# Banded attention of a two-block transformer kernel: single heads in a row against batches of four heads

## The reference

```
WINDOW = 128; SWA_Q_HEADS = 8; SWA_KV_HEADS = 2; SWA_GROUP = 4; HEAD_DIM = 64
kb, vb = band(k), band(v)        # own block of 128 keys and the one before
s = einsum('bnqhgd,bnkhd->bnhgqk', qb, kb) * (HEAD_DIM ** -0.5) + bias
s = where(mask, s, NEG_INF)      # banded and causal
p = softmax(concatenate([s, sink], axis=-1), axis=-1)[..., :-1]
o = einsum('bnhgqk,bnkhd->bnqhgd', p, vb)
```

## Time and profile before

| | us |
|---|---|
| median of 3 runs (2503.61 to 2506.11) | 2503.81 |
| span of the profiled execution, first to last instruction | 2500.4 |
| median less span | 3.4 |
| banded attention, first weight load of its scores (269.08) to first weight load of the dense scores (358.25) | 89.17 |
| PE, DVE and ACT busy in it | 79.26, 81.90, 52.35 |

### The profile page before, as it was taken

How to read it: one execution, slowest core, us unless ns; L and a number is a source line. 1 busy time by engine, 2 the same in 40 slices (tenths; PEclk the granted TensorE clock), 3 DMA queues, 4 the chain that set the end, 5 groups by cost and what they waited for, 6 DMA issues and landing times.

```text
span 2500.4 us, 32413 instructions
## 1 busy us (share of the span) xinstructions
PE 2411.0 (96%) x11302; PEld 1886.2 (75%) x11302; DVE 1599.2 (64%) x2478; ACT 1248.2 (50%) x1874; POOL 751.4 (30%) x396
## 2 busy tenths in 40 slices
PE   8999899999999999999999999999997999999996
PEld 6587567778788878878788778766764878878885
DVE  4033887756563357675442734687247999999998
ACT  4111555434543432443333411377245888888887
POOL 0312100114444477334466331120311132123310
PEclk9999999999999999999999999999998999999998
DMA  6210000022222264222233211000438999999996
GB/s 241 98 49 3 35 1 1 1 101 87 91 93 101 95 241 151 84 85 91 93 118 112 73 61 40 34 1 1 153 141 309 402 395 388 380 391 385 392 390 234
DMA packets 86602, 384.08 MB, mean 154 GB/s; under 512 B 7980, under 2 KB 9180, under 8 KB 71520
## 3 DMA queue, kind: packets, MB, share of 16 engines
q1 hardware_dynamic: 81744, 365.25, 38.7%
q0 software_dynamic: 4752, 17.43, 2.6%
HBM read 361.60 MB, written 21.05 MB: 153 GB/s over the span
## 4 chain that ended last, share of the span: by engine, by line
PE 49%; issue 11%; DVE 7%; POOL 4%; ACT 2%; DMA 1%; SPq 0%; POOLq 0%; DVEq 0%; ACTq 0%
PE ps L997 10%; PE ps L999 9%; PE ps L998 9%; PE ps L1367 5%; PE ps L1369 5%; PE ps L1368 5%; POOL w_lo L2816 4%; DVE e_lo L2672 3%; PE ps L1202 2%; PE ps L1192 1%; DMA arena<-in_w_gate 1%; PE ps L1274 1%; PE ps L1403 1%; DMA residual_rows<-arena 0%; PE ps L1181 0%
## 5 line engine op out<-in xcount | busy, mean ns | idle before, releaser
L2816 POOL TENSOR_TENSOR w_lo<-arena,w_hi 128x1024 fp32r<-128x1024 f32 x188 | 457.5, 2434 | 702.4 <-ACT w_hi L1608 700.1
L2672 DVE TENSOR_TENSOR e_lo<-arena,e_hi 128x1024 fp32r<-128x1024 f32 x384 | 451.3, 1219 | 35.4 <-ACT e_hi L1940 30.6
L1940 ACT ACTIVATE e_hi<-arena 128x1024 fp32r<-128x1024 f32 x384 | 401.3, 1059 | 88.1 <-PE ps L1369 82.0
L1608 ACT ACTIVATE w_hi<-arena 128x1024 fp32r<-128x1024 f32 x188 | 198.4, 1055 | 367.0 <-PE ps L999 366.9
L997 PE MATMUL ps<-h_hi,w_hi 128*128 128x512 f32 x848 | 336.4, 397 | 8.4 <-POOL w_lo L2816 5.3
L999 PE MATMUL ps<-h_hi,w_lo 128*128 128x512 f32 x848 | 332.0, 391 | 0.0
L998 PE MATMUL ps<-h_lo,w_hi 128*128 128x512 f32 x848 | 331.7, 391 | 0.0
L1367 PE MATMUL ps<-e_hi,x_hi 128*128 128x512 f32 x512 | 205.0, 400 | 7.2 <-DVE e_lo L2672 4.4
L1369 PE MATMUL ps<-e_lo,x_hi 128*128 128x512 f32 x512 | 200.2, 391 | 0.0
L1368 PE MATMUL ps<-e_hi,x_lo 128*128 128x512 f32 x512 | 200.0, 391 | 0.0
L997 PEld LDWEIGHTS ps<-h_hi,w_hi 128*128 128x128 f32 x848 | 160.4, 189 | 48.5 <-issue 12.2
(11 more groups left out here) (388 smaller groups left out, 5091.2 us busy)
## 6 DMA issues: line engine op xcount, KB each, us to landing
arena<-in_w_up SPq DMA_DIRECT2D x108, 1024.0 KB, 8.0
arena<-in_w_down SPq DMA_DIRECT2D x86, 1024.0 KB, 7.7
arena<-in_w_gate SPq DMA_DIRECT2D x64, 1024.0 KB, 10.0
arena<-in_w_in SPq DMA_DIRECT2D x18, 1024.0 KB, 4.8
arena<-in_w_out SPq DMA_DIRECT2D x16, 1024.0 KB, 4.8
arena<-in_w_ada SPq DMA_DIRECT2D x12, 1024.0 KB, 13.7
arena<-in_w_ada SPq DMA_DIRECT2D x24, 512.0 KB, 6.7
routed_rows<-arena SPq DMA_DIRECT2D x8, 520.0 KB, 7.5
```

Of the source, the lines that this page charges most:

```text
L1608: act_e.activation(w_hi[:, q, :], slot[c][:, q * D:(q + 1) * D], ACT.Copy).then_inc(s_whi, 1)
L1940: act_e.activation(e_hi[:, (2 * sl + a) % RING, :], slot[sl][:, a * D:(a + 1) * D], ACT.Copy).then_inc(s_ehi, 1)
L2672: v.tensor_tensor(e_lo[:, r, :], slot[sl][:, a * D:(a + 1) * D], e_hi[:, r, :].bitcast(F32), ALU.subtract).then_inc(s_elo, 1)
L2816: gp.tensor_tensor(w_lo[:, q, :], slot[c][:, q * D:(q + 1) * D], w_hi[:, q, :].bitcast(F32), ALU.subtract).then_inc(s_wlo, 1)
```

## The change

The banded attention leaves `units` and gets code of its own, in 16 batches of four heads: batch b is block b // 2 with key head b % 2, heads 4 (b % 2) to 4 (b % 2) + 3.

- Scores go into half a bank each, banks 0 and 1 for even batches, 2 and 3 for odd ones, two batches ahead of the turned rows.
- `sw_raw` holds four rows of 257 elements. POOL writes the sinks once into the first column of each (two copies of 128x4, with a wait, ahead of its clearing of `qs`). DVE writes the biased scores behind it. The exponential runs over 257 columns from `sw_raw` to `sw_probs`, so that its sum holds the sink; line 1559 and line 2226 are gone in this stage.
- The turned rows of four heads fill bank 4 (first 128 keys) and bank 5 (second 128 keys). ACT copies bank 4 out (`swa_near_out`, 128x512), DVE copies bank 5 (`swa_far_out`, 128x512, only where there are 256 keys).
- The values of a batch are 16 PE instructions in a row (8 in block 0), into bank 6 + b % 2. DVE takes four reciprocals at once and scales the 128x256 output with one instruction (`swa_out`).
- PE's sequence is written out, without the loop.
- `sw_turned` lies where the first `w_out` slot is, so SP issues the `w_out` loads only after the values of the last batch.
- The first dense unit's scores come before the values of batch 15.

```diff
         ropeq = view(52, S)
         wukv = view(6, 512)
 
-        gsq = [[view(24 + 2 * i, 512) for i in range(2)], [view(96 + i, 256) for i in range(NT)], [view(192 + i, 256) for i in range(4)]]
+        sw_raw = [view(kb, 4 * 257).rearrange("p (a b) -> p a b", a=4) for kb in (16, 20.015625)]
+        sw_probs = [view(kb, 4 * 257).rearrange("p (a b) -> p a b", a=4) for kb in (176, 180.015625)]
+        sw_turned = [[view(4 * b + 2 * j, HALF) for j in range(2)] for b in range(2)]
+        gsq = [[view(28 + 2 * i, 512) for i in range(2)], [view(96 + i, 256) for i in range(NT)], [view(192 + i, 256) for i in range(4)]]
         convm = view3(176, 4, S)
         late_probs = [view(64, S), view(68, S)]
         band = view(164, 320).bitcast(BF16)
...
@@ -465,6 +465,14 @@
 
         HEAD_ROWS = [slice(0, HD), slice(HD, P)]
 
+        def sw_keys(b):
+
+            return 2 * P if b >= 2 else P
+
+        def sw_scores(b, c):
+
+            return ps[:, 2 * (b % 2) + c // 2, c % 2 * 256:c % 2 * 256 + sw_keys(b)]
+
         PAIRS = [(m, half) for ms in (range(4), (4, 5)) for half in range(2) for m in ms] + [(6, 0), (7, 0)]
         TURN_AT = {8 + 5: 0, 8 + 7: 1, 16 + 3: 2, 16 + 5: 3, 16 + 7: 4, 24 + 3: 5, 24 + 5: 6, 24 + 7: 7, 48 + 3: 8, 48 + 5: 9, 48 + 7: 10, 56 + 3: 11}
...
@@ -566,6 +570,7 @@
                     sp.dma_start(slot[(g0 + n - 1) % 2], src[:, n - 1, :]).then_inc(s_wl[(g0 + n - 1) % 2], 16)
 
             out1 = T["w_out"].rearrange("p (g n) -> p g n", n=ITEM)
+            sp.wait_ge(s_pv, U_DENSE)
             for g in range(KT):
                 if g >= 2:
                     sp.wait_ge(s_wlo, 2 * (G_OUT + g) - 2)
...
@@ -921,26 +924,40 @@
             pe.wait_ge(s_krc, 1)
             pe.wait_ge(s_frow, 16)
 
-            def swa(n, par):
-                nk = P if isinstance(n, int) and n == 0 else 2 * P
-
-                def keys():
-                    if nk == P:
-                        return swak[:, 0:P]
-                    return swak[:, bass.ds(n * P - P, nk)]
-
-                def scores(u):
-                    if u == 0:
-                        pe.wait_ge(s_stage, n + 1)
-                    return pe.matmul(ps[:, 2 * (u % 2), 0:nk], qs[par][:, u // 2 + 4 * (u % 2), :], keys(), start=True, stop=True)
-
-                def values(u, j):
-                    c = HD * (u % 2)
-                    if nk == P:
-                        return swav[:, 0, c:c + HD]
-                    return swav[:, bass.ds(n + (j - 1), 1), c:c + HD].rearrange("p a c -> p (a c)")
-                return scores, lambda u: nk, values
-
+            def swa_scores(b, cs):
+
+                n, g, w = b // 2, b % 2, sw_keys(b)
+                if cs[0] == 0:
+                    pe.wait_ge(s_stage, n + 1)
+                if b >= 2:
+                    pe.wait_ge(s_max, 4 * (b - 2) + cs[-1] + 1)
+                for c in cs:
+                    m = pe.matmul(sw_scores(b, c), qs[n % 2][:, 4 * g + c, :], swak[:, (n + 1) * P - w:(n + 1) * P], start=True, stop=True)
+                    if c % 2:
+                        m.then_inc(s_S, 2)
+
+            def swa_turned(b, cs):
+
+                if cs[0] == 0 and b:
+                    pe.wait_ge(s_pt, 4 * b)
+                for c in cs:
+                    pe.wait_ge(s_exp, 4 * b + c + 1)
+                    for j in range(sw_keys(b) // P):
+                        m = pe.transpose(ps[:, 4 + j, c * P:(c + 1) * P], sw_probs[b % 2][:, c, 1 + j * P:1 + (j + 1) * P], ident)
+                if cs[-1] == 3:
+                    m.then_inc(s_T, 4)
+
+            def swa_values(b):
+
+                n, g, nb = b // 2, b % 2, sw_keys(b) // P
+                pe.wait_ge(s_pt, 4 * b + 4)
+                if b >= 2:
+                    pe.wait_ge(s_o, 4 * (b - 1))
+                for c in range(4):
+                    for j in range(nb):
+                        m = pe.matmul(ps[:, 6 + b % 2, c * HD:(c + 1) * HD], sw_turned[b % 2][j][:, c * P:(c + 1) * P], swav[:, n + 1 - nb + j, g * HD:(g + 1) * HD],
+                                      start=(j == 0), stop=(j == nb - 1))
+                m.then_inc(s_pv, 4)
 
             def dense(h, par):
                 def scores(u):
@@ -957,11 +974,16 @@
                     return VH[:, j, bass.ds(h * HD, HD)]
                 return scores, lambda u: (u + 1) * P, values
 
-            units(U_SWA, swa(0, 0))
-            units(8, swa(1, 1), swa(0, 0))
-            with pe.Fori(1, NT // 2) as m:
-                for b in range(2):
-                    units(m * 16 + 8 * b, swa(2 * m + b, b), swa(2 * m + (b - 1), 1 - b))
+            swa_scores(0, range(4))
+            swa_scores(1, range(4))
+            for b in range(2 * NT):
+                for cs in (range(2), range(2, 4)):
+                    swa_turned(b, cs)
+                    if b + 2 < 2 * NT:
+                        swa_scores(b + 2, cs)
+                if b < 2 * NT - 1:
+                    swa_values(b)
+
             def pair_turned(p):
 
                 k, half = PAIRS[p]
...
@@ -1549,18 +1571,11 @@
                 g = T_LV + t
                 half1(g, (VH[:, 2 * t + 1, 256:512], ps[:, b1(g), 0:256])).then_inc(eva, 2 if t == 3 else 1)
 
-            def exps(n, g, cols_of, src, probs=probs, layer=None, hooks={}):
+            def exps(n, g, cols_of, src, hooks={}):
 
                 for u in range(n):
                     act_e.wait_ge(s_max, g + (u + 1))
-                    if layer is not None:
-                        if not isinstance(g, int) or g + u >= 4:
-                            act_e.wait_ge(s_o, g + (u - 3))
-                        act_e.activation(sden[:, u % 4:u % 4 + 1], sinkcol(layer, u), ACT.Exp, bias=nmax[:, u % 4:u % 4 + 1], scale=-1.0).then_inc(s_sx, 1)
                     w, c = cols_of(u), u % 4
-                    if layer is not None:
-                        act_e.activation(probs[u % 2][:, 0:w], probs[u % 2][:, 0:w], ACT.Exp, bias=nmax[:, c:c + 1], scale=-1.0, accum_out=den[:, c:c + 1]).then_inc(s_exp, 1)
-                        continue
                     if not isinstance(g, int) or g + u >= 2:
                         act_e.wait_ge(s_T, g + (u - 1))
@@ -1595,11 +1610,33 @@
                     act_e.wait_ge(s_stage, NT + CH)
                 act_e.activation(mixed_part(m, half, 0), pair_columns(), ACT.Copy, scale=col("group", m)).then_inc(eva, 1)
 
-            for n in range(NT):
-                w = 2 * P if n else P
-                exps(8, 8 * n, lambda u: w, None, probs, 0)
-                if n:
-                    group_square(0, n - 1, 8 * n)
+            def swa_exp(b, c):
+
+                i, w = 4 * (b % 2) + c, sw_keys(b) + 1
+                act_e.wait_ge(s_max, 4 * b + c + 1)
+                if b >= 2 and c == 0:
+                    act_e.wait_ge(s_T, 4 * (b - 1))
+                    act_e.wait_ge(s_o, 4 * (b - 1))
+                act_e.activation(sw_probs[b % 2][:, c, 0:w], sw_raw[b % 2][:, c, 0:w], ACT.Exp, bias=sw_nmax[:, i:i + 1], scale=-1.0,
+                                 accum_out=sw_den[:, i:i + 1]).then_inc(s_exp, 1)
+
+            def swa_near_out(b):
+
+                act_e.wait_ge(s_T, 4 * b + 4)
+                if b >= 2:
+                    act_e.wait_ge(s_pv, 4 * (b - 1))
+                act_e.activation(sw_turned[b % 2][0], ps[:, 4, :], ACT.Copy).then_inc(s_pt, 2 if b >= 2 else 4)
+
+            act_e.wait_ge(s_ssi, 2)
+            for b in range(2 * NT):
+                swa_exp(b, 0)
+                if b:
+                    swa_near_out(b - 1)
+                for c in range(1, 4):
+                    swa_exp(b, c)
+                if b % 2 and b > 1:
+                    group_square(0, b // 2 - 1, 8 * (b // 2))
+            swa_near_out(2 * NT - 1)
 
             def weight_high(gg, c, q, free):
...
@@ -2205,12 +2242,7 @@
                     if now:
                         c = u % 4
                         v.wait_ge(s_S, g + (u + 1))
-                        if now[3] is None:
-                            v.tensor_reduce(nmax[:, c:c + 1], now[0](u), AX_X, ALU.max, negate=True).then_inc(s_max, 1)
-                        else:
-                            after(s_T, -1, u, 2)
-                            v.tensor_tensor_reduce(probs[u % 2][:, 0:now[1](u)], now[0](u), now[4](u), -1.0, sinkcol(now[3], u),
-                                                   ALU.add, ALU.min, nmax[:, c:c + 1]).then_inc(s_max, 1)
+                        v.tensor_reduce(nmax[:, c:c + 1], now[0](u), AX_X, ALU.max, negate=True).then_inc(s_max, 1)
                     w = u - 1
                     if (now or u == 0) and group(w):
                         v.wait_ge(s_T, g + (w + 1))
...
-                        v.tensor_scalar(group(w)[2](w % 8), ps[:, value_bank(w, g + w >= U_DENSE), 0:HD], rec[:, c:c + 1], None, ALU.mult).then_inc(s_o, 1)
+                        v.tensor_scalar(group(w)[2](w % 8), ps[:, 6, 0:HD], rec[:, c:c + 1], None, ALU.mult).then_inc(s_o, 1)
```

(35 more changed lines are left out.)

42 lines of the change are left out of this document (22 added, 20 removed).

## The result

The changed kernel takes 2484.32 us (median of 4 runs, 2482.36 to 2486.95) where the kernel before, run beside it, takes 2503.71 (2499.09 to 2506.11). The ratio is 0.9927 with a 95% interval of 0.9912 to 0.9942. That is 0.73% faster, and the predicted time was 2484.3. The span of the profiled execution went from 2500.4 to 2481.5 us. For the medians (19.4 us apart here, 18.7 in the later comparison) no run shows where the rest came from.

What follows compares the result with a forecast made beforehand. DVE's work per head was taken as the bound, with a hand-over to ACT and PE behind it. Stage terms gave 89.2 - 68.3 - 1.4 = 19.5 us, so 2503.8 - 19.5 = 2484.3 us; range 2479 to 2496.

Steps and rivals of the forecast that it cites:

- The bound and who takes it over: Banded attention stage: DVE's work per head sets the pace before; batching takes DVE off the path, PE becomes longest.
- PE's own work per batch: Turned rows 0.88, scores 1.70 and values 1.76 us on PE, together 4.34 us per batch of four heads.
- The wait: PE ahead of each batch's values, until DVE's copy of turned rows is done: 0.22 us per batch.
- The period: Time per batch in batches 2 to 13: values begin at 2.80 us and take 1.76, so 4.56 us.
- The start: Stage opening: PE starts about 0.3 us later, then eight scores take 1.8 us, in which the first exponentials are done.
- The middle and the end: Batches 0 and 1 at 3.2 us each, 2 to 13 at 4.56, batch 14 at 4.2, batch 15 at 0.9.
- The sum: 68.3 us to the first dense load against 89.17, with 1.4 given back after it: net gain 19.5 us.
- The 3.4 us: Whole program: the median lies 3.4 us above the profiled execution of 2500.4 us, and that distance is kept.
- Hand-overs: Rival, chance 0.13: DVE's copy starts late in each batch, the wait grows by up to 0.85 us, program 2496 us.
- PE full at 2494: Rival, chance 0.05: by busy time PE idles only 9.9 us of the stage, so the program ends at 2494 us.
- Given back later: Rival, chance 0.05: a fixed-time transfer, or a stage waiting for one, returns the gain; program 2503.8 us.
- The clock: Rival, chance 0.04: PE's bursts drop the clock to 1.2 GHz for about half its stage work; program 2517 us.

Runs made afterwards that it cites:

- the later comparison: The changed kernel timed once more, unedited, beside the kernel before: median 2484.74 us (2481.67 to 2493.5), ratio 0.9924.
- the lagging kernel: The changed kernel with values made one batch later on PE and output one batch later on DVE: stage 65.5 us, median 2480.64 us, ratio 0.9905.

## Why the prediction was right

**The bound and who takes it over: right.** DVE fell out of the path and PE became the bound. PE's own work per batch was put at 4.34 us and the lagging kernel shows 4.34. The wait was put at 0.22 us, ended by DVE's copy, and is 0.25, ended by DVE's copy. The period was 4.56 and is 4.58 to 4.59, one batch of the twelve excepted: its values start 4.77 us behind those before, released by ACT's copy, which began 0.28 us after DVE's. Why is open.

**The start: one term missed.** I had the turned rows begin 1.8 us after the first score load. They begin 3.16 us after it (269.73 to 272.89), and 1.17 us of that is PE's wait behind the table load. The step that failed is "eight scores, in which the first exponentials are done". The kernel before had its table load out of the way, and I didn't ask what it stands behind now. POOL's two copies cost POOL 0.38 us and PE 0.2: from the start of `keep_clock` to the first score load it is 4.93 us before and 5.13 after, where the prediction had 0.3 more. The first score load is 0.65 us later on the clock of the trace, but 0.45 of that was there ahead of the stage (`keep_clock` starts at 264.15 and 264.60).

**The middle and the end: right.** Batches 0 and 1 took 6.5 us (6.4 in the prediction), batch 14 4.2 as said, batch 15 0.88 to the dense load, and the second dense maximum follows 3.8 us after it (3.6).

**The sum: 2.1 us too large.** By the second dense maximum the lead is 360.43 - 343.49 = 16.9 us, and by the first read of `w_out` 403.0 - 385.9 = 17.1. Counted from the start of `keep_clock`, so without the 0.45 us that were lost ahead of the stage, the change gave 17.4 us, where the sum had 19.5. Of the 2.1 us the late table load is 1.4, batches 2 to 13 are 0.5 (0.02 to 0.03 us each, and the odd one), and batches 0 and 1 and the end 0.3; POOL's smaller cost gives 0.1 back.

**What made it come out even: the clock elsewhere.** The kernel before had a low-clock stretch in its 3.30 us window at 535; the kernel after had none in its first execution there. On either side of that window the lead goes from 17.1 us (first weight load of line 998, 1020 after, at 534.6 and 517.5) to 18.7 (first load of `h_lo` there, 633.6 and 614.9). Later it is as much as 19.8, which was not followed up, and 18.9 at the end of the two profiles. More such stretches lie differently from execution to execution, and move the end by several us either way. The prediction gave them "1 or 2 us", which is too little. The executions of the changed kernel reach from 2481.67 to 2493.5. The 3.4 us that the prediction put around the span are 1.9 in the runs since, where both numbers are on record (2483.35 against 2481.5); the remaining 1.5 are most likely a profiled execution faster than the median, and they drop out of the difference.

**The rivals.** Hand-overs: not here, but eight DVE instructions in place of two ahead of the copy cost 9 us, so DVE's cover was as thin as was said. PE full at 2494: refuted, the same matmuls fit into a stage of 64.4 us. Given back later: refuted, the two profiles are 17 us apart at the first read of `w_out` and 18.9 at the end. The clock: I argued from the small waits of the middle batches, 0.22 us, and those are harmless. But I had put waits of about 1.6 and 0.9 us for batches 14 and 15 into my own sum without asking the same of them. The first of them takes the clock in some executions and costs 4.0 us there. The Trainium skill (TensorE: Matmul & The Clock Gate, A second HAM failure mode: psum-queue depth-cycling) speaks of brief idling between groups of matmuls that throttles the clock, and the run with one batch of lead agrees with that sentence, at a mean of 0.86 with waits of 2.1 us per batch. The middle of the changed kernel, at 1.00 with 0.38, doesn't show it, and neither does the run with the output scaled per head, at 1.00 with 0.95.

## What to carry to other kernels

Count what each engine has to issue from start to start, not its busy time; here the new period followed from the longest of them plus the one hand-over that nothing covers. When work is put in batches, ask whether the lead has to grow with the batch (here one batch of lead made it a loss), and what stands in a queue ahead of a shared copy, which mattered more here than that engine's total. Look at the first and the last batch by themselves, for a table load that has slipped behind a wait and for waits long enough to cost the clock of the next stage.

## What the runs showed of the hardware

- A table load of ACT took 1.28 us and can stand behind a semaphore wait of the activation that it serves. With one wait on that activation, for the maximum, it ran early; with two it began after the maximum, and PE waited 1.17 us.
- The granted clock fell to 1.2 GHz about 2 us after the end of a single wait of 1.57 us on PE, with work in between, and in another execution of the same kernel it did not fall. Over the profiles with two batches of lead it fell there in five of six with a wait of 1.56 us or more and in none of five without. Waits of 0.95 us in every batch of 5.15 us left it at 1.00, waits of 2.1 us in every batch brought means of 0.86 and 0.88.
- An fp32 matmul of 256 columns costs PE 0.43 us from start to start, a weight load of 128x128 in a run of them 0.11, and a batch built from these prices came out at the 4.34 us that was counted.
